# Attention values with the probabilities stationary: the product computed untransposed, scaled from PSUM and transposed once

## Chip, cores, metric

One core of a Trainium2 chip runs the whole kernel as one program. The metric is device time in microseconds, from launch to end; the median of three runs stands for a kernel. A profile is one execution recorded by the hardware profiler; its span runs from the first to the last instruction. PE is TensorE (PEld its weight loads), DVE VectorE, ACT ScalarE, POOL GpSimd, SP SyncE. All data is fp32; a matmul operand marked fp32r is an fp32 value rounded for the faster matmul form.

## What is computed

Two transformer-like models in a row on 512 tokens of width 1024. Four attention stages matter here, three kinds of token attention and one cross-attention into 256 memory tokens; the rest are projections, feed-forward blocks and a delta-rule stage. The stages differ in their scores and masks and end alike:

```python
def windowed_gqa(q, k, v, sink):           # 12 heads, blocks of 128 queries, 256 or 384 keys
...
    p = jax.nn.softmax(jnp.concatenate([s, sink_col], axis=-1), axis=-1)[..., :-1]
    o = jnp.einsum('bkgniu,bnukd->bnikgd', p.astype(v.dtype), vband)
def neighbourhood_attn(q, k, v, rpb):      # 12 heads, all 512 keys, a bias per pair of positions
...
    o = jnp.einsum('bhrcij,brijhd->brchd', p.astype(v.dtype), vband)
def memory_attn(q, k, v):                  # 4 heads, 256 memory keys
...
    o = jnp.einsum('bhsm,bmhd->bshd', p.astype(v.dtype), v)
def swa_mixer(h, wq, wk, wv, q_norm_w, k_norm_w, sinks, wo):   # 16 heads, 16 meta tokens first
...
    orr = (jnp.einsum('bnkgim,bmkd->bnikgd', p[..., :N_META], vm)
           + jnp.einsum('bnkgij,bnjkd->bnikgd', p[..., N_META:], vband))
```

The head width is 64. The result of each stage goes through an output projection.

## The kernel before

Activations lie transposed, features on partitions and tokens along the row. Large matmuls run in three passes of rounded halves (`h_hi`, `h_lo` against `w_hi`, `w_lo`, L949 and L962); attention values and transposes run in plain fp32.

An attention stage works on *pairs*: two heads of one feature tile and one block of queries. A pair is numbered by `count`; `slot` is its parity. Layer 0 has 24 pairs of windowed attention (blocks of 2, 3, 3 and 2 chunks of 128 keys) and 8 pairs of memory attention (2 chunks); layer 1 has 24 pairs of neighbourhood attention (4 chunks) and 8 memory pairs; the last layer has 40 pairs (8 tiles of 5 blocks: one of 16 queries by 16 keys, one of 128 + 16 keys, three of 128 + 128 + 16 keys).

Each engine has its own program, in an order written out by hand, and meets the others only through semaphores. The stage is a software pipeline: in step *p* PE does the scores of pair *p* (L1031), the values of pair *p*-2 (L1060) and the transposes of the probabilities of pair *p*-1 (L1044). A plain fp32 matmul is issued as two passes, each with its own weight load, so a chunk of values costs two passes per head, a transpose one.

For the values of a pair (`values`) PE keeps the values `v_st` (n keys by 64 columns) stationary and streams the transposed probabilities `p_t` (128 queries): the output has features on partitions, head 0 on partitions 0 to 63 and head 1 on 64 to 127 of PSUM bank 6 or 7. The reciprocals of the row sums lie with queries on partitions, so they must be turned as well: DVE computes `p_inv` (L1252), ACT spreads it to 64 columns a head (`spread`, L758, into `p_rec`), PE transposes it into the other half of the bank (L1064) and only then raises `pv_done`. ACT then copies the product to SBUF (`move_y`, L766, into `y_sb`), DVE multiplies it by the reciprocals in PSUM (`normalise`, L1237), ACT rounds the result into `h_hi` (`y_hi`, L771) and POOL computes the remainder `h_lo` (L579), which the output projection waits for. POOL also stages queries, keys and values for the next tile.

PE's step waits for `s_read` (scores bank free), `pt_ready` (probabilities turned and copied), `y_ready` (bank 6 or 7 free, a pair two earlier) and `rec_ready`. ACT's step is `move_y(p-2)`, `y_hi(p-3)`, and twice `turned(p-1)` and `probs(p)`, then `spread(p-1)`. DVE's step is the scale, bias and row maximum of pair *p* (L1232 or L1242, L1257), the reciprocal of *p*-1 and `normalise(p-2)`.

## Time and profile before

| | us |
|---|---|
| median of three runs | 3296.27 (3291.29 to 3299.48) |
| span of the profiled execution | 3296.4 |
| PE busy in it | 2886.2 (88%) |
| DVE, ACT, POOL busy | 1329.9, 981.6, 1204.4 |

The five attention stretches in the profiled execution, from their first score to the next stage's first matmul, read from the timeline: layer 0 tokens 174 to 254 us, memory 254 to 278; layer 1 tokens 888 to 984, memory 984 to 1008; last layer 2620 to 2812.6. The granted TensorE clock has two levels in this profile, shown as 1.00 (2.4 GHz) and 0.50 (1.2 GHz) of full speed; a stretch that holds both shows a mean. How to read a row of the stretch table: busy time and instruction count of each engine inside the stretch, then the mean granted clock.

### The profile page before, as it was taken

What the parts mean: (1) busy time and instruction counts of PE and PEld (TensorE: products, weight loads), DVE (VectorE), ACT (ScalarE), POOL (GpSimd) and SP (SyncE); (2) the same over time, 40 slices, a digit from 0 to 9 for tenths busy, and PEclk for the clock granted to TensorE, in tenths of its full rate; (3) what the DMA queues carried; (4) which work ended last, traced back from release to release, by engine and by line L of the source; (5) the groups of instructions that cost most, each with busy time, mean ns of one, the idle gap of its engine ahead of it and who ended that gap; (6) DMA issues with size and microseconds to landing.
All of it is one profiled execution on the core that took longest, in us unless ns stands there. A gap on an engine that the chain in (4) does not pass through costs nothing.

```text
span 3296.4 us, 50250 instructions
## 1 busy us (share of the span) xinstructions
PE 2886.2 (88%) x18018; PEld 2530.7 (77%) x18018; DVE 1329.9 (40%) x1506; ACT 981.6 (30%) x1863; POOL 1204.4 (37%) x727
## 2 busy tenths in 40 slices
PE   6898899989998999979966667999998699899998
PEld 5766778767976778759955556999998466799998
DVE  2265321341275322354724444653642233464361
ACT  3264212221284222232441113222222454322221
POOL 3443444434453434424321103433434132343342
PEclk7999999989999999989967787999998755899999
DMA  4211222322231222322200001222222000122222
GB/s 129 69 44 47 75 88 90 99 73 77 53 54 51 83 93 85 99 68 71 83 26 0 0 0 51 72 87 84 91 81 64 20 1 1 51 83 85 86 90 77
DMA packets 80355, 212.78 MB, mean 65 GB/s; under 512 B 30224, under 2 KB 32912, under 8 KB 80272
## 3 DMA queue, kind: packets, MB, share of 16 engines
q1 hardware_dynamic: 80272, 211.69, 21.0%
q8 instruction: 49, 0.80, 0.1%
q14 instruction: 34, 0.28, 0.0%
HBM read 209.57 MB, written 2.10 MB: 64 GB/s over the span
## 4 chain that ended last, share of the span: by engine, by line
PE 75%; DVE 8%; issue 7%; ACT 4%; POOL 4%; DVEq 1%; DMA 0%; POOLq 0%; ACTq 0%; SPq 0%
PE ps L949 56%; PE ps L1060 5%; PE ps L962 4%; PE ps L1136 3%; PE ps L1044 2%; POOL w_lo L486 2%; PE ps L1031 2%; DVE normed L1232 2%; POOL h_lo L620 2%; PE ps L1121 1%; DVE sq_sum L1237 1%; PE ps L1064 1%; DVE act_lo L1237 1%; ACT h_hi L726 1%; DVE n_max L1257 1%
## 5 line engine op out<-in xcount | busy, mean ns | idle before, releaser
L486 POOL TENSOR_TENSOR w_lo<-raw,w_hi 128x1024 fp32r<-128x1024 f32 (+1 forms) x352 | 896.6, 2549 | 1339.7 <-ACT w_hi L685 1339.7
L949 PE MATMUL ps<-h_hi,w_hi 128*128 128x264 f32 (+2 forms) x3120 | 826.8, 321 | 46.4 <-POOL w_lo L486 29.4
L685 ACT ACTIVATE w_hi<-raw 128x1024 fp32r<-128x1024 f32 (+1 forms) x352 | 392.4, 1116 | 1521.4 <-PE ps L949 1365.6
L949 PE MATMUL ps<-h_lo,w_hi 128*128 128x264 f32 (+2 forms) x3120 | 828.6, 322 | 0.0
L949 PE MATMUL ps<-h_hi,w_lo 128*128 128x264 f32 (+2 forms) x3120 | 826.8, 321 | 0.0
L949 PEld LDWEIGHTS ps<-h_hi,w_hi 128*128 128x128 f32 x3120 | 524.4, 191 | 95.1 <-POOL w_lo L486 32.8
L949 PEld LDWEIGHTS ps<-h_lo,w_hi 128*128 128x128 f32 x3120 | 522.2, 190 | 42.3
L949 PEld LDWEIGHTS ps<-h_hi,w_lo 128*128 128x128 f32 x3120 | 522.7, 191 | 41.5
L949 PE MATMUL ps<-act_hi,w_hi 128*128 128x264 f32 (+1 forms) x1056 | 289.6, 329 | 51.9 <-DVE act_lo L1237 51.9
L949 PE MATMUL ps<-act_lo,w_hi 128*128 128x264 f32 (+1 forms) x1056 | 289.1, 329 | 0.0
L949 PE MATMUL ps<-act_hi,w_lo 128*128 128x264 f32 (+1 forms) x1056 | 288.3, 328 | 0.0
L1237 DVE TENSOR_TENSOR x<-x,ps 128x512 f32 (+1 forms) x96 | 66.8, 696 | 474.6 <-PE ps L949 474.6
L949 PEld LDWEIGHTS ps<-act_hi,w_hi 128*128 128x128 f32 x1056 | 181.1, 194 | 71.0 <-POOL w_lo L486 54.3
L1060 PE MATMUL ps<-p_t,v_st 128*64 128x128 f32 (+1 forms) x1136 | 198.8, 332 | 12.6 <-ACT p_t L747 7.3
L1237 DVE TENSOR_TENSOR prod<-silu_g,ps 128x512 f32<-128x512 f32 (+1 forms) x88 | 61.3, 697 | 356.2 <-PE ps L949 303.7
L949 PEld LDWEIGHTS ps<-act_lo,w_hi 128*128 128x128 f32 x1056 | 181.3, 195 | 16.5
L949 PEld LDWEIGHTS ps<-act_hi,w_lo 128*128 128x128 f32 x1056 | 180.9, 194 | 16.0
L1237 DVE TENSOR_TENSOR sq_sum<-sq_sum,sq 128x512 f32<-128x512 f32 (+2 forms) x80 | 167.5, 2094 | 57.2 <-ACT sq L693 54.7
L1060 PEld LDWEIGHTS ps<-p_t,v_st 128*64 128x64 f32 (+1 forms) x1136 | 132.8, 162 | 73.7 <-issue 45.6
L1237 DVE TENSOR_TENSOR act_lo<-prod,act_hi 128x512 f32 (+1 forms) x88 | 155.0, 1761 | 22.1 <-DVE act_hi L1247 22.1
L1242 DVE TENSOR_SCALAR conv<-padded,vec 128x528 f32<-128x528 f32 x56 | 102.3, 1827 | 108.2 <-ACT padded L808 104.4
L1247 DVE CAST act_hi<-prod 128x512 f32 (+1 forms) x88 | 131.5, 1495 | 18.0 <-DVE prod L1237 18.0
(196 smaller groups left out, 3439.1 us busy)
## 6 DMA issues: line engine op xcount, KB each, us to landing
raw<-slabs_d SPq DMA_DIRECT2D x288, 512.0 KB, 3.5
raw<-slabs_d SPq DMA_DIRECT2D x64, 704.0 KB, 4.1
rpb_raw<-rpb_d SPq DMA_DIRECT2D x24, 224.0 KB, 5.0
bias_sb<-alibi_d SPq DMA_DIRECT2D x6, 384.0 KB, 3.3
x<-x_d SPq DMA_DIRECT2D x1, 2048.0 KB, 12.4
out_d<-x SPq DMA_DIRECT2D x1, 2048.0 KB, 7.0
mem_in<-mem_d SPq DMA_DIRECT2D x1, 1024.0 KB, 6.0
dn_cst<-dn_consts_d SPq DMA_DIRECT2D x1, 640.0 KB, 5.7
```

What stands on the lines that cost most here:

```text
L486: nc.gpsimd.tensor_tensor(w_lo[:, s, 0:size * P], raw[:, s, 0:size * P], w_hi[:, s, 0:size * P].bitcast(f32), ALU.subtract).then_inc(lo_do ...
L620: nc.gpsimd.tensor_tensor(h_lo[:, k, t], normed[:, k % 2, t], h_hi[:, k, t].bitcast(f32), ALU.subtract).then_inc(h_ready, 1)
L685: nc.scalar.activation(w_hi[:, s, 0:size * P], raw[:, s, 0:size * P], ACT.Copy).then_inc(hi_done, 1)
L949: last = nc.tensor.matmul(ps[:, s * 2 * BANK + po:s * 2 * BANK + po + n], w[:, s, wk], a[:, k, to:to + n], start=(k == 0 and w is w_hi and ...
L962: last = nc.tensor.matmul(out, a[:, k, t0:t0 + n], w[:, s, wk], start=(k == 0 and w is w_hi and a is h_hi), stop=(k == DT - 1 and w is w_lo))
L1031: last = nc.tensor.matmul(bank(2 * p.slot + h)[0:p.nq, col:col + n], a[hp, p.tile_slot, p.q], b[hp, p.tile_slot, k0:k0 + n], start=(b is k ...
L1044: last = nc.tensor.transpose(bank(4 + h)[0:n, j * P:j * P + p.nq], s_sb[0:p.nq, p.slot, h, 1 + col:1 + col + n], ident[0:p.nq, 0:p.nq])
L1060: nc.tensor.matmul(out[HD * h:HD * h + HD, 0:p.nq], v_st[0:n, p.tile_slot, vb, HD * h:HD * h + HD], p_t[0:n, h, j, 0:p.nq], start=(j == 0) ...
L1136: last = nc.tensor.matmul(out[:, h, :], lhs(h), rhs(h), start=start, stop=stop)
L1237: return nc.vector.tensor_tensor(*a, **kw)
L1242: return nc.vector.tensor_scalar(*a, **kw)
L1247: return nc.vector.tensor_copy(*a, **kw)
```

## The change

`values` swaps its operands: the transposed probabilities (n keys by 128 queries) are stationary and the values (64 columns) are streamed, so that the product has queries on partitions and both heads side by side. DVE multiplies it straight out of PSUM by `p_inv`, broadcast along each head's 64 columns, into `y_rows`; PE transposes `y_rows` once into the second half of the same bank (`turn_y`); ACT rounds that from PSUM into `h_hi`, and DVE, no longer POOL, computes `h_lo` from PSUM. `spread`, `move_y`, `p_rec`, `y_sb` and POOL's part are gone.

```diff
@@ POOL, attend @@
-                    pool.wait_ge(y_hi_ready, k + 1)
-                    nc.gpsimd.tensor_tensor(h_lo[:, st.y + i, q], y_sb[:, (i * nb + b) % 2, 0:c["nq"]],
-                                            h_hi[:, st.y + i, q].bitcast(f32), ALU.subtract).then_inc(y_lo_ready, 1)
@@ ACT, attend @@
-                def spread(p):
...
-                def move_y(p):
...
                 def y_hi(p):
-                    act.wait_ge(y_ready, p.count + 1)
-                    nc.scalar.activation(h_hi[:, st.y + p.tile, p.q], y_sb[:, p.slot, 0:p.nq],
+                    act.wait_ge(y_turned, p.count + 1)
+                    nc.scalar.activation(h_hi[:, st.y + p.tile, p.q], bank(6 + p.slot)[:, P:P + p.nq],
                                          ACT.Copy).then_inc(y_hi_ready, 1)
@@ PE, attend @@
                     if counted(p.count - 1):
-                        pe.wait_ge(y_ready, p.count - 1)
+                        pe.wait_ge(y_lo_ready, p.count - 1)
...
-                            nc.tensor.matmul(out[HD * h:HD * h + HD, 0:p.nq],
-                                             v_st[0:n, p.tile_slot, vb, HD * h:HD * h + HD],
-                                             p_t[0:n, h, j, 0:p.nq], start=(j == 0), stop=(j == len(cs) - 1))
-                    pe.wait_ge(rec_ready, p.count + 1)
-                    nc.tensor.transpose(out[:, P:P + p.nq],
-                                        p_rec[0:p.nq, p.slot, :],
-                                        ident[0:p.nq, 0:p.nq]).then_inc(pv_done, 1)
+                            last = nc.tensor.matmul(out[0:p.nq, HD * h:HD * h + HD],
+                                                    p_t[0:n, h, j, 0:p.nq],
+                                                    v_st[0:n, p.tile_slot, vb, HD * h:HD * h + HD],
+                                                    start=(j == 0), stop=(j == len(cs) - 1))
+                    last.then_inc(pv_done, 1)
+
+                def turn_y(p):
+                    pe.wait_ge(y_scaled, p.count + 1)
+                    nc.tensor.transpose(bank(6 + p.slot)[:, P:P + p.nq], y_rows[0:p.nq, p.slot, :],
+                                        ident[0:p.nq, 0:p.nq]).then_inc(y_turned, 1)
 
                 def step(p):
                     scores(p)
+                    if p.back(3).exists:
+                        turn_y(p.back(3))
                     if p.back(2).exists:
                         values(p.back(2))
@@ DVE, attend @@
-                    if counted(p.count - 1):
-                        wait(rec_ready, p.count - 1)
...
                 def normalise(p):
-                    wait(y_moved, p.count + 1)
-                    y = y_sb[:, p.slot, 0:p.nq]
-                    tt(y, y, bank(6 + p.slot)[:, P:P + p.nq], ALU.mult).then_inc(y_ready, 1)
+                    wait(pv_done, p.count + 1)
+                    wait(inv_ready, p.count + 1)
+                    tt(y_rows[0:p.nq, p.slot, :].rearrange("p (h n) -> p h n", h=2),
+                       bank(6 + p.slot)[0:p.nq, 0:P].rearrange("p (h n) -> p h n", h=2),
+                       p_inv[0:p.nq, p.slot, :].unsqueeze(2).to_broadcast([p.nq, 2, HD]),
+                       ALU.mult).then_inc(y_scaled, 1)
+
+                def y_lo(p):
+                    wait(y_hi_ready, p.count + 1)
+                    tt(h_lo[:, st.y + p.tile, p.q], bank(6 + p.slot)[:, P:P + p.nq],
+                       h_hi[:, st.y + p.tile, p.q].bitcast(f32), ALU.subtract).then_inc(y_lo_ready, 1)
...
+                    if p.back(3).exists:
+                        y_lo(p.back(3))
```

PE in a step of the windowed stage of layer 0 (scores of a pair with 256 keys, values of one with 3 chunks, transposes of one with 3 chunks); each values row is issued as two passes. Before:

```order
L1031 MATMUL ps<-k_hi,q_hi 128x256 [waits s_read]
L1031 MATMUL ps<-k_hi,q_hi 128x256
L1031 MATMUL ps<-k_lo,q_hi 128x256 x2
L1031 MATMUL ps<-k_hi,q_lo 128x256 x2
L1060 MATMUL ps<-p_t,v_st 64x128 [waits pt_ready]
L1060 MATMUL ps<-p_t,v_st 64x128 x2
L1060 MATMUL ps<-p_t,v_st 64x128 [waits pt_ready]
L1060 MATMUL ps<-p_t,v_st 64x128 x2
L1064 MATMUL ps<-cst,p_rec 128x128 [waits rec_ready]
L1044 MATMUL ps<-cst,s_sb 128x128 [waits pt_ready,p_ready]
```

And the same step of the changed kernel (L990 is the line of the scores, L1019 of the values, L1003 of the transposes, L1027 of `turn_y`):

```order
L990 MATMUL ps<-k_hi,q_hi 128x256 [waits s_read]
L990 MATMUL ps<-k_hi,q_hi 128x256
L990 MATMUL ps<-k_lo,q_hi 128x256 x2
L990 MATMUL ps<-k_hi,q_lo 128x256 x2
L1027 MATMUL ps<-cst,y_rows 128x128 [waits y_scaled]
L1019 MATMUL ps<-v_st,p_t 128x64 [waits pt_ready]
L1019 MATMUL ps<-v_st,p_t 128x64 x2
L1019 MATMUL ps<-v_st,p_t 128x64 [waits pt_ready]
L1019 MATMUL ps<-v_st,p_t 128x64 x2
L1003 MATMUL ps<-cst,s_sb 128x128 [waits pt_ready,p_ready]
```

The one transpose moved from behind the values to ahead of them and now belongs to a pair one step older; the values' output shape went from 64x128 to 128x64, in the same number of matmuls.

DVE in one step of the same stage, before:

```order
L1237 TENSOR_TENSOR s_sb<-rows 128x2 [waits pt_done]
L1232 SCALAR_TENSOR_TENSOR s_sb<-ps,bias_sb 128x2x384 [waits s_done]
L1257 TENSOR_REDUCE n_max<-s_sb 128x2
L1252 RECIPROCAL p_inv<-p_sum 128x2 [waits rec_ready,p_ready]
L1237 TENSOR_TENSOR y_sb<-y_sb,ps 128x128 [waits y_moved]
```

And of the changed kernel:

```order
L1204 TENSOR_TENSOR s_sb<-rows 128x2 [waits pt_done]
L1199 SCALAR_TENSOR_TENSOR s_sb<-ps,bias_sb 128x2x384 [waits s_done]
L1224 TENSOR_REDUCE n_max<-s_sb 128x2
L1219 RECIPROCAL p_inv<-p_sum 128x2 [waits p_ready]
L1204 TENSOR_TENSOR h_lo<-ps,h_hi 128x128 [waits y_hi_ready]
L1204 TENSOR_TENSOR y_rows<-ps,p_inv 128x128 [waits inv_ready,pv_done]
```

A sixth instruction came in ahead of the last one, and the last one waits for PE where it waited for ACT.

## Rows read from the trace of the kernel before

**Rows 1.** The page: granted TensorE clock in 40 equal slices, tenths.

```profile
PEclk7999999989999999989967787999998755899999
```

**Rows 2.** Stretches: busy us (instructions) of each engine, granted clock, DMA.

```profile
186.00:254.00 68.00, 63.10 (x487) 46.75 (x485) 47.07 (x105) 53.92 (x196) 30.56 (x48) 1.00 0.22 53
254.00:257.40 3.40, 1.27 (x13) 0.68 (x12) 2.76 (x4) 1.91 (x7) 3.23 (x6) 1.00 0.00 0
257.40:260.80 3.40, 3.40 (x21) 2.52 (x21) 2.00 (x5) 2.33 (x9) 0.85 (x2) 0.50 0.04 10
260.80:277.00 16.20, 14.86 (x116) 10.40 (x114) 9.61 (x22) 13.40 (x56) 2.75 (x6) 1.00 0.00 1
899.10:984.00 84.90, 84.18 (x715) 67.19 (x714) 62.09 (x89) 70.92 (x205) 50.81 (x58) 1.00 0.33 57
...
2636.50:2646.80 10.30, 9.61 (x76) 6.39 (x74) 4.86 (x16) 6.56 (x33) 6.32 (x11) 1.00 0.00 0
2646.80:2812.60 165.80, 162.42 (x722) 102.87 (x720) 59.46 (x167) 78.07 (x360) 39.69 (x76) 0.50 0.00 1
2812.60:2817.40 4.80, 4.77 (x22) 4.80 (x23) 0.00 (x0) 0.00 (x0) 0.00 (x0) 0.50 0.01 3
```

**Rows 3.** Stretches, L1105 alone (loads 128 columns, streams 8): PE, PEld, clock.

```profile
1670.00:1674.00 4.00, 4.00 (x38) 4.00 (x37) 0.99 0.00 0
1674.00:1684.50 10.50, 10.50 (x51) 10.50 (x51) 0.50 0.00 0
```

**Rows 4.** Timeline, layer 1, PE: start, us, instruction, count [idle before <- releaser].

```profile
932.10 0.33 PE L1064 MATMUL ps<-cst,p_rec 128*128 128x128 f32 x1
...
934.13 1.70 PE L1060 MATMUL ps<-p_t,v_st 128*64 128x128 f32 x16
935.76 0.33 PE L1064 MATMUL ps<-cst,p_rec 128*128 128x128 f32 x1
```

**Rows 5.** Timeline, layer 1, DVE in the same step.

```profile
934.28 1.23 DVE L1232 SCALAR_TENSOR_TENSOR s_sb<-ps,bias_sb 128x1024 f32<-128x1024 f32 x1 [0.38 <-PE ps L1031]
...
937.30 0.29 DVE L1237 TENSOR_TENSOR y_sb<-y_sb,ps 128x128 f32<-128x128 f32 x1
```

**Rows 6.** Timeline, layer 0, PE's transposes of the reciprocals in three steps.

```profile
219.45 0.33 PE L1064 MATMUL ps<-cst,p_rec 128*128 128x128 f32 x1
...
222.82 0.33 PE L1064 MATMUL ps<-cst,p_rec 128*128 128x128 f32 x1
...
225.79 0.33 PE L1064 MATMUL ps<-cst,p_rec 128*128 128x128 f32 x1
```

**Rows 7.** Timeline, layer 0, DVE: the first instruction of two successive steps.

```profile
218.54 0.16 DVE L1237 TENSOR_TENSOR s_sb<-rows 128x2 f32 x1 [0.17 <-issue]
...
221.80 0.16 DVE L1237 TENSOR_TENSOR s_sb<-rows 128x2 f32 x1 [0.17 <-issue]
```

**Rows 8.** Timeline, memory attention of layer 0, PE.

```profile
262.07 0.33 PE L1064 MATMUL ps<-cst,p_rec 128*128 128x128 f32 x1
264.68 0.33 PE L1064 MATMUL ps<-cst,p_rec 128*128 128x128 f32 x1
```

**Rows 9.** Chain that ended last, last layer: start, us, engine, tile, line, count.

```profile
2630.12 2.46 PE ps L1060 x8
...
2648.08 2.46 PE ps L1060 x8
...
2668.99 0.32 ACT s_sb L735 x2
...
2671.95 2.46 PE ps L1060 x8
...
2677.08 3.32 PE ps L1060 x12
...
2682.26 3.32 PE ps L1060 x12
```

**Rows 10.** Timeline, end of the last layer's attention, ACT's copy of the last product.

```profile
2810.65 0.28 ACT L766 ACTIVATE y_sb<-ps 128x128 f32<-128x128 f32 x1 [3.10 <-PE ps L1064]
```

More of the change, by code:

```diff
@@ L782, in step @@
                         probs(p, h)
-                    if p.back(1).exists:
-                        spread(p.back(1))
                 over_pairs(act.Fori, st, step)
                 last = last_pair(st)
-                move_y(last.back(1))
                 y_hi(last.back(2))
@@ L790, in attend @@
                     turned(last, h)
-                spread(last)
-                move_y(last)
                 y_hi(last.back(1))
@@ L1083, in attend @@
                 last = last_pair(st)
+                turn_y(last.back(2))
                 values(last.back(1))
                 turn(last)
+                turn_y(last.back(1))
                 values(last)
+                turn_y(last)
             def ffn(st):
@@ L1385, in attend @@
                 invert(last)
+                y_lo(last.back(2))
                 normalise(last.back(1))
+                y_lo(last.back(1))
                 normalise(last)
+                y_lo(last)
             def residual(q0, blk, squares):
```

47 lines of the change are left out of this document (11 added, 36 removed).

## The prediction

> **What bounds the kernel now.** I read the page first, then the stretch table, then single steps on the timeline. The page's clock line [rows 1] is near full speed except in three places; the 31st to 34th slice are the last layer's attention and what leads to it. The change touches only the attention steps, 104 pairs in about 410 of the 3296 us, so everything is decided there.
>
> PE bounds them, but at two clocks. In the token attention of layers 0 and 1 the clock is 1.00 and PE is busy 63.1 of 68.0 and 84.2 of 84.9 us. In the last layer it is 0.50 for 165.8 us although PE is busy 162.4 of them [rows 2]. So a busy PE does not raise the clock by itself; it matters what it does. The memory stage of layer 0 shows both directions: in the gap between two stages (PE busy 1.27 of 3.40) the clock falls, PE then works through 3.40 us at half clock, and the clock is back.
>
> **What a pass costs.** Today a pass of values loads 64 columns and streams 128; afterwards it loads 128 and streams 64. L1105 shows such a load-heavy pass: 128 columns of a 4-byte operand loaded, 8 streamed. At clock 0.99 it made 38 passes in 4.00 us (0.105 each), at 0.50 51 in 10.5 us (0.206) [rows 3]. Today's values pass costs (1.70 - 0.27) / 15 = 0.095 us at full clock, with some overlap of the two heads [rows 4]. So the halved stream buys nothing: the load of 128 columns takes its place, at both clocks. I take 0.105 and 0.21 for a pass of the changed kernel; from below the bound would be half of each (the stream alone), and rows 3 speak against that.
>
> The Trainium skill (TensorE: Matmul & The Clock Gate, section on LDWEIGHTS) gives a load as columns / 1.2 ns, whatever the clock: 107 ns for 128 columns. At full clock rows 3 agree; at half clock they show 206. By the page the last layer would save 0.1 us on each of its 352 full passes, 35 us.
>
> The count of passes stays: a values pass for a values pass, `turn_y` for the reciprocals' transpose. In layers 0 and 1 one change of the array's shape per step goes, about 0.1 us, and layer 1 loses the overlap of the two heads, 16 x (0.105 - 0.095), about 0.16. PE's work per step is the same within 0.1 us.
>
> **What happens to the clock.** This is the term that decides. L1105 loads full width, streams 8 columns, is back to back, busy 4.00 of 4.00 us, and the clock falls within it and stays at 0.50 for 10.5 us of unbroken work [rows 3]. Loads, then, do not hold the clock; streaming does. The change halves what the values stream: a memory pair streams (8 x 128 + 5 x 128 + scores) today and (8 x 64 + 5 x 128 + scores) afterwards. The last layer's pairs, with a third of their values passes on 16 rows, stream little for their time and stay at half clock for 165.8 us. Afterwards memory pairs and two-chunk pairs of layer 0 are in the last layer's place: when a gap between stages has dropped the clock, I expect nothing to raise it before the output projection. Three-chunk pairs may raise it, four-chunk pairs (layer 1) should.
>
> The Trainium skill (the same page, Part 1) says that sustained matmul activity releases the throttle and that idle time brings it back. By that rule a PE that never idles would keep the full clock after the change too: it is the first rival below. The last layer contradicts it (162.4 of 165.8 us busy at 0.50) and so does L1105.
>
> **Price of a pair at half clock.** A three-block step of the last layer takes 2682.26 - 2677.08 = 5.18 us [rows 9] for 19 passes (12 values, 6 transposes, 1 reciprocals): 19 x 0.21 = 4.0; three scores of 272 columns at 1.2 GHz, 0.68; the rest, 0.5, are six changes of the array's shape. With two changes left, a pair of layer 0 with 3 chunks costs 4.0 + 0.96 + 0.16 = 5.1, one with 2 chunks 13 x 0.21 + 0.64 + 0.16 = 3.5, one of layer 1 25 x 0.21 + 1.28 + 0.16 = 6.7. Today they take 3.37 and 2.97 (mean 3.17) [rows 6], a memory pair 2.61 [rows 8], a pair of layer 1 935.76 - 932.10 = 3.66 [rows 4].
>
> **The sum**, against the profiled 3296.4, which is the median within 0.2:
>
> 1. Layer 0 tokens: half clock for none to all of 24 pairs, each (5.1 + 3.5) / 2 - 3.17 = +1.15: 0 to 28. I take half of them: **+13.8**.
> 2. Two memory stages: 8 x (3.5 - 2.61) = 7.3, less 0.9 for the 3.4 us that already run at half clock, less about 1 for pairs of the stage's start and end that wait anyway: 5.5 each, **+11**.
> 3. The output projections behind them then start at half clock, as the last layer's does now for 4.8 us [rows 2]: half of that, twice, **+4.8**.
> 4. Layer 1 tokens: 3.4 us more at half clock after the start, x (1 - 3.66 / 6.7): **+1.6** (0 to 40, were it never to rise).
> 5. The last layer loses its one stretch at full clock, 10.3 us [rows 2]. The period that holds it took 2648.08 - 2630.12 = 17.96, the next 23.87 [rows 9]: **+5.9**.
> 6. DVE gets `y_lo`, 0.29 us by the row of the same shape, and a wait before it (0.1 to 0.25), less one wait in the reciprocal: +0.4 a step. In layer 1 DVE's chain is 937.30 + 0.29 - 934.28 = 3.31, with 0.1 to the next start 3.4, and it waits 0.38 for PE [rows 5]; with 3.8 it is longer than PE's 3.66: 24 x 0.15 = **+3.6**. In layer 0 its step with 384 keys takes 3.26 [rows 7] of 3.37; with 3.66 it adds 0.29 on the six such pairs still at full clock: **+1.7**. At half clock DVE is hidden behind PE. Ends: 0 (the added operation hides in the wait) and 12.
> 7. ACT loses `spread` and `move_y`, some 0.5 us a step. In layer 0 its step and PE's transpose of the reciprocals form the loop of 3.37, so PE is released from it; DVE's 3.66 takes over. In the last layer ACT stands on the chain for 0.32 us once in a period [rows 9], 8 periods, of which I credit 0.25: **-2**. At the end of a stage that a projection follows, the chain loses the copy, 0.28 us [rows 10], and a hop between engines, about 0.2: thrice, **-1.5**. POOL's release gains nothing: PE waits for it only at a stage's start.
>
> Together +38.9: **3335 us**, 1.2% slower.
>
> **The rivals.**
>
> A. *The clock holds* in layers 0 and 1 and the memory stages (the page's rule, or a margin larger than I think). For it: four-chunk pairs have much to give away, and today's memory stage regains the clock after one 3.4 us stretch. Against it: rows 3 and the last layer. Then terms 1 to 4 vanish, term 6 is 3.6 + 12 x 0.29 = 7, term 5 perhaps stays: 3296 + 7 + 6 - 3.5 = 3306 down to 3300. Chance 0.12.
>
> B. *Full-width loads are cheap at half clock* (the page's figure for LDWEIGHTS) while the clock falls as forecast: 35 us come back in the last layer and about 10 in the other half-clock pairs: 3335 - 40 = 3295, no change. Chance 0.05.
>
> C. *Both*: the clock holds and loads hide. At full clock DVE bounds anyway, so the last layer's 35 us are the gain: 3303 - 35 = 3268. Chance 0.07.
>
> D. *DVE's early link*: PE now waits for `y_scaled` of pair p-3 right behind the scores, where it waited for a product a whole step older. If that ties PE's step to DVE's (3.8 and 3.7 plus two hops of 0.2 in two steps, 3.95 each), layer 1 adds 24 x 0.15 more and layer 0 about 2: 3340, inside the forecast's range. It decides only where DVE's step is as long as PE's, not at half clock.
>
> E. *Layer 1 falls too* and stays at half clock: + up to 24 x 3.0 = 72, near 3400. Its pairs still stream most of all attention pairs. Chance 0.04.
>
> **Chances and range.** The forecast with D's variant has 0.72, and by its own ends (term 1 from 0 to 28, the rest as summed) runs from 3315 to 3360. The rest is A 0.12, B 0.05, C 0.07, E 0.04. The range 3300 to 3360 takes in A and leaves C and E out. A measurement of this kernel tells about 0.3% (10 us, so 3286 and 3306) from no change. Faster is C with a sliver of B: 0.08. Same is A and B: 0.15. Slower is the forecast and E: 0.77.
>
> **What the profile of the changed kernel would show.** Term 1 to 4: the stretches of layer 0, above all both memory stages, with a granted clock of 0.50 and PE busy nearly throughout; the output projections' first microseconds at 0.50. Term 5: no stretch at 1.00 between the last layer's first score and its projection. The pass: values with 0.21 us from start to start at half clock, 0.105 at full; 0.11 at half clock would prove B. Term 6: in layer 1 DVE busy nearly without waiting for PE, steps of 3.8 us. I am wrong if the memory stages run at 1.00 (then 3300 to 3306) or if layer 1's steps are shorter than 3.66 us.

## The result and the profile after

The changed kernel takes 3352.83 us (median of 4, 3348.04 to 3356.12), the kernel before 3293.94 beside it: a ratio of 1.0172, 95% interval 1.0158 to 1.0186. It is 1.7% slower, 58.9 us by the medians and 57.9 by the spans of the two profiled executions (3354.3 against 3296.4). The forecast was 38.9 us. Two of the ten executions of a later kernel (e5) took 3302.0 and 8825.3 us at a lower granted clock (0.897 and 0.298, against 0.912 to 0.918) and are left out of its ratio.

The page of the changed kernel, granted TensorE clock in 40 slices, answers [rows 1]:

```profile
PEclk7875999998997999998986778899998755799999
```

The third and fourth slice, where layer 0's attention and its projection stand, are new, and so is the 7 in the thirteenth, layer 1's memory stage. The next view gives the five attention stretches, from the first score of a stage to its last product: us, then for each engine busy time and instructions, granted clock, DMA share, GB/s. First the kernel before, cut at the same places (layer 0 tokens, layer 0 memory, layer 1 tokens, layer 1 memory, last layer):

```profile
174.50:253.30 78.80, 71.52 (x530) 52.82 (x530) 55.55 (x119) 59.59 (x214) 39.95 (x55) 0.96 0.19 46
253.30:277.50 24.20, 20.71 (x153) 14.43 (x152) 14.65 (x32) 18.11 (x72) 6.91 (x13) 0.93 0.01 2
889.30:983.10 93.80, 90.12 (x746) 71.47 (x746) 69.30 (x95) 74.79 (x214) 60.11 (x65) 0.98 0.30 51
983.10:1007.60 24.50, 20.66 (x153) 14.54 (x152) 14.64 (x32) 18.11 (x72) 6.90 (x13) 0.93 0.00 1
2619.80:2810.60 190.80, 183.71 (x856) 116.96 (x856) 75.60 (x198) 90.65 (x421) 55.35 (x98) 0.53 0.02 6
```

And the changed kernel:

```profile
181.70:284.70 103.00, 95.89 (x528) 81.48 (x528) 62.25 (x143) 51.04 (x168) 33.45 (x38) 0.62 0.15 35
284.70:317.80 33.10, 31.03 (x153) 26.07 (x152) 17.00 (x40) 15.27 (x57) 0.00 (x0) 0.50 0.00 1
930.10:1036.40 106.30, 96.04 (x746) 80.08 (x746) 76.36 (x119) 64.21 (x168) 54.04 (x48) 0.97 0.27 45
1036.40:1069.10 32.70, 30.30 (x152) 25.46 (x152) 17.01 (x40) 15.27 (x56) 0.00 (x0) 0.54 0.00 1
2677.40:2870.60 193.20, 187.77 (x856) 145.79 (x856) 85.61 (x238) 75.23 (x344) 40.22 (x60) 0.50 0.02 6
```

Two different losses stand side by side. In layer 0 and in both memory stages TensorE is busy nearly all the time, at a lower clock: +24.2, +8.9 and +8.2 us. In the tokens of layer 1 the clock is what it was (0.97), and TensorE is idle 10.3 us of 106.3 where it was idle 3.7 of 93.8: +12.5 us. Not all of that is waiting: TensorE's busy time there rose by 5.9 us (90.12 to 96.04), at nearly the same clock, because its passes and steps are a little longer; e5 below shows what that costs. The last layer, at half clock before as well, adds 2.4. The two output projections take 46.2 and 46.0 us instead of 44.7 each, since they start at half clock: +2.8.

One more difference has nothing to do with attention. A stretch of 96 passes of the memory keys and values, the same in both kernels, ran at full clock before and mostly at half after (before, then after):

```profile
60.00:71.00 11.00, 10.92 (x96) 10.78 (x96) 0.47 (x2) 1.40 (x2) 4.75 (x2) 1.00 0.39 103
60.00:78.20 18.20, 18.10 (x96) 17.91 (x95) 0.49 (x2) 1.27 (x3) 4.73 (x2) 0.57 0.24 87
```

That is 7.3 us in this one execution. Of the twelve kernels run later, with the same code there, one (e5) shows it slow and eleven fast. So it belongs to the execution, and the change's own loss in the profile is nearer to 50 than to 58 us. The medians can't be corrected for it, as each kernel has a profile of one execution only.

In layer 0 the clock does not stay down from the stage's start. From 193.7 to 211.7 us it is at 1.00, with TensorE busy 14.6 of 18.0 us, and it falls to 0.50 at about 216 us, inside the stage and with no gap between stages before it. It stays there for the 68.7 us that are left of the tokens and through the memory stage.

A pass at half clock costs what rows 3 said. TensorE, changed kernel, memory stage of layer 0 (start, us, line, form, count), answers [rows 8]:

```profile
297.55 0.48 PE L1027 MATMUL ps<-cst,y_rows 128*128 128x128 f32 x1
297.82 1.81 PE L1019 MATMUL ps<-v_st,p_t 128*128 128x64 f32 x8
299.42 1.06 PE L1003 MATMUL ps<-cst,s_sb 128*128 128x128 f32 x4
...
301.35 0.48 PE L1027 MATMUL ps<-cst,y_rows 128*128 128x128 f32 x1
```

Eight value passes from 297.82 to 299.42 are 0.20 us each, and the pair takes 301.35 - 297.55 = 3.80 us (2.61 before, 3.5 forecast). In layer 1 at full clock (answers [rows 4]):

```profile
962.90 0.33 PE L1027 MATMUL ps<-cst,y_rows 128*128 128x128 f32 x1
963.08 2.00 PE L1019 MATMUL ps<-v_st,p_t 128*128 128x64 f32 x16
...
967.43 0.33 PE L1027 MATMUL ps<-cst,y_rows 128*128 128x128 f32 x1 [0.59 <-DVE y_rows L1204]
```

and VectorE over two steps, from 959.21 on (answers [rows 5]):

```profile
959.21 1.22 DVE L1199 SCALAR_TENSOR_TENSOR s_sb<-ps,bias_sb 128x1024 f32<-128x1024 f32 x1 [0.20 <-PE ps L990]
...
961.84 0.17 DVE L1219 RECIPROCAL p_inv<-p_sum 128x2 f32<-128x2 f32 x1
962.10 0.29 DVE L1204 TENSOR_TENSOR h_lo<-ps,h_hi 128x128 fp32r<-128x128 f32 x1
...
963.32 1.23 DVE L1199 SCALAR_TENSOR_TENSOR s_sb<-ps,bias_sb 128x1024 f32<-128x1024 f32 x1 [0.48 <-PE ps L990]
964.64 1.22 DVE L1224 TENSOR_REDUCE n_max<-s_sb 128x2 f32<-128x1024 f32 x1
966.07 0.17 DVE L1219 RECIPROCAL p_inv<-p_sum 128x2 f32<-128x2 f32 x1 [0.21 <-issue]
966.63 0.29 DVE L1204 TENSOR_TENSOR h_lo<-ps,h_hi 128x128 f32 x1 [0.40 <-issue]
967.08 0.29 DVE L1204 TENSOR_TENSOR y_rows<-ps,p_inv 128x128 f32<-128x128 f32 x1 [0.16 <-issue]
967.64 1.23 DVE L1199 SCALAR_TENSOR_TENSOR s_sb<-ps,bias_sb 128x1024 f32<-128x1024 f32 x1 [0.27 <-issue]
```

Two VectorE steps take 967.64 - 959.21 = 8.43 us, 4.2 each, where TensorE's step was 3.66. The last 3.0 us of them hold no wait for another engine, and TensorE waits 0.59 us for what comes out of them. The first of the two steps still belongs to the group that the kernel writes out ahead of its loop, the second to the loop. The remainder `h_lo` follows the reciprocal within 0.1 us in the first and after 0.40 us in the second.

Two theories come out of this, and they need not exclude each other. **Clock**: the value passes stream half the columns, and that is what lost the clock. **VectorE**: with the remainder in its sequence VectorE sets the step at full clock. A variant of it says that it is the place of `y_rows` in the chain, not the length of the sequence (rival D of the prediction).

### The profile page after: what moved, and what is told of

It is laid out like the page before. It is cut to its first block, busy times and chain, and to the rows that moved or that the text cites. A ratio compares the mean times of both kernels' runs of the same rounds, so it can differ in the third digit from the quotient of the medians.

```text
span 3354.3 us, 49859 instructions
## 1 busy us (share of the span) xinstructions
PE 2943.8 (88%) x18018; PEld 2623.1 (78%) x18018; DVE 1357.5 (40%) x1610; ACT 939.8 (28%) x1655; POOL 1159.4 (35%) x623
## 4 chain that ended last, share of the span: by engine, by line
PE 75%; DVE 9%; issue 7%; ACT 4%; POOL 4%; DVEq 1%; DMA 0%; POOLq 0%; ACTq 0%; SPq 0%
PE ps L908 55%; PE ps L1019 5%; PE ps L921 4%; PE ps L1103 3%; PE ps L1003 2%; PE ps L990 2%; POOL w_lo L485 2%; DVE normed L1199 2%; POOL h_lo L602 2%; PE ps L1088 1%; DVE sq_sum L1204 1%; DVE n_max L1224 1%; DVE s_sb L1199 1%; PE ps L1027 1%; DVE act_lo L1204 1%
## 5 line engine op out<-in xcount | busy, mean ns | idle before, releaser
L1019 PE MATMUL ps<-v_st,p_t 128*128 128x64 f32 (+1 forms) x1136 | 227.2, 361 | 4.7 <-ACT p_t L731 4.5
L1019 PEld LDWEIGHTS ps<-v_st,p_t 128*128 128x128 f32 (+1 forms) x1136 | 212.1, 270 | 21.8 <-issue 5.3
```

The source lines that it names most:

```text
L1019: last = nc.tensor.matmul(out[0:p.nq, HD * h:HD * h + HD], p_t[0:n, h, j, 0:p.nq], v_st[0:n, p.tile_slot, vb, HD * h:HD * h + HD], start=( ...
```

## The experiments

Ratios are to the kernel before, run beside each kernel. Its medians in the four sets were 3297.0, 3298.3, 3297.6 and 3298.3 us, so the kernels' times can be compared across sets.

### e1: the columns of both heads

```diff
-                            last = nc.tensor.matmul(out[0:p.nq, HD * h:HD * h + HD],
+                            last = nc.tensor.matmul(out[0:p.nq, P * (2 + h):P * (3 + h)],
                                                     p_t[0:n, h, j, 0:p.nq],
-                                                    v_st[0:n, p.tile_slot, vb, HD * h:HD * h + HD],
+                                                    v_st[0:n, p.tile_slot, vb, :],
```

(and `normalise` reads the half of each head that counts)

> The changed kernel, with one thing else: each value pass streams the 128 columns of both heads' values instead of the 64 of its own head, and the half that belongs to the other head is left unread. The number of passes and what they load stay. Theory (the clock): the pairs of layer 0 and of both memory stages ran at half clock (granted clock 0.50 from 216 to 289 and from 289 to 318.8 us in the changed kernel) because the value passes stream half the columns; with 128 columns again these stretches are back at 1.00 for the most part, a pass still takes about 0.11 us at full clock (16 in 2.00 us), layer 0's attention takes 105 to 115 us instead of 136.0, and the kernel 3305 to 3325. What is left above the kernel before is the chain over VectorE. Rival (the clock goes by the time that TensorE is busy, or by passes): the half-clock stretches stay where they are and the kernel is within 8 us of 3353. Second rival: twice the columns make a pass longer; then 16 value passes of layer 1 take over 3 us and the kernel is slower than 3353.

Measured: **3314.0 us** (ratio 1.0048, 1.0033 to 1.0063), 38.8 below the changed kernel and 17.0 above the kernel before. The profiled execution is the slowest of its ten (3324.3 us, granted clock 0.899 where most had 0.903), so some 10 us of the stretches below are not in its median; which stretch holds them is not known. The five stretches again:

```profile
174.10:264.10 90.00, 66.28 (x528) 54.91 (x528) 64.15 (x143) 51.93 (x168) 33.41 (x38) 0.96 0.17 40
264.10:290.60 26.50, 20.82 (x153) 16.81 (x152) 17.02 (x40) 15.18 (x56) 0.00 (x0) 0.87 0.01 1
901.50:1006.40 104.90, 95.38 (x744) 79.74 (x744) 76.38 (x119) 64.17 (x168) 54.07 (x48) 0.98 0.28 46
1006.40:1032.40 26.00, 19.88 (x153) 16.27 (x152) 17.02 (x40) 15.19 (x56) 0.00 (x0) 0.93 0.00 1
2641.40:2838.50 197.10, 190.20 (x856) 136.22 (x856) 86.54 (x238) 74.73 (x343) 40.24 (x60) 0.56 0.02 6
```

Layer 0's attention, 116.5 us with its memory stage, just misses the forecast of 105 to 115. The instructions are the same in number, but for a few records that the traces miss. Only what each value pass streams, and writes to PSUM, has doubled, and the clock is back, from 0.62 to 0.96, 0.50 to 0.87 and 0.54 to 0.93. At full clock a pass costs hardly more: 16 take 1.88 us (933.03 to 934.91 on the timeline) where the changed kernel's take 1.74 to 1.83. At half clock it costs 0.03 us more, 8 in 1.86 us (269.23 to 271.09) for 1.60, and so the last layer, which stays near half clock, gets 3.9 us longer (197.1 for 193.2). So the columns streamed (with what they write) are the cause, not busy time and not the number of passes or loads: TensorE was busy 95.89 of 103.0 us at a clock of 0.62 and is busy 66.28 of 90.0 at 0.96. This speaks directly against the rule of the Trainium skill (TensorE: Matmul & The Clock Gate, Part 1) that the clock goes by how busy TensorE has been, if busy is what the profile counts as busy.

What is left above the kernel before, 90.0 against 78.8 us in layer 0's tokens and 104.9 against 93.8 in layer 1's, is now visible without the clock. VectorE in layer 0 of e1:

```profile
203.08 0.16 DVE L1204 TENSOR_TENSOR s_sb<-rows 128x2 f32 x1 [0.18 <-issue]
203.39 0.96 DVE L1199 SCALAR_TENSOR_TENSOR s_sb<-ps,bias_sb 128x768 f32<-128x768 f32 x1
204.44 0.95 DVE L1224 TENSOR_REDUCE n_max<-s_sb 128x2 f32<-128x770 f32 x1
205.55 0.17 DVE L1219 RECIPROCAL p_inv<-p_sum 128x2 f32<-128x2 f32 x1 [0.16 <-issue]
205.94 0.29 DVE L1204 TENSOR_TENSOR h_lo<-ps,h_hi 128x128 f32 x1 [0.22 <-issue]
206.47 0.29 DVE L1204 TENSOR_TENSOR y_rows<-ps,p_inv 128x128 f32<-128x128 f32 x1 [0.23 <-issue]
206.94 0.16 DVE L1204 TENSOR_TENSOR s_sb<-rows 128x2 f32 x1 [0.18 <-issue]
```

It waits for no engine at all. The step is 206.94 - 203.08 = 3.86 us; [rows 7] has 3.26 for the same step before. VectorE is the bound there, and TensorE waits for it: in the stage's 90.0 us it waits 21 times, 21.1 us in all, at `turn_y` for `y_rows`.

### e2 and e3: the transpose of the rows behind the values

```diff
                     scores(p)
-                    if p.back(3).exists:
-                        turn_y(p.back(3))
                     if p.back(2).exists:
                         values(p.back(2))
+                    if p.back(3).exists:
+                        turn_y(p.back(3))
```

(and on VectorE `normalise(p-2)` ahead of `y_lo(p-3)`); e2 on the changed kernel, e3 on e1.

> The changed kernel, in another order: TensorE transposes the scaled rows of pair p-3 behind the value passes of pair p-2 instead of ahead of them, and VectorE scales pair p-2 before it takes the remainder of pair p-3. The same instructions. Theory (the chain over VectorE costs about 10 us in layer 1: there, at full clock, PE sat idle 0.4 to 0.6 us before each transpose of y_rows, and the stretch of 84.9 us became 95.6): the idle time ahead of that transpose goes, layer 1 loses 8 to 10 us, and the kernel takes 3341 to 3347. Layer 0, at half clock, has no such idle time and stays at 136 us. Rival (VectorE's own added work, not its place in the chain, sets the step of layer 1): the idle time moves to another instruction and the kernel stays at 3350 to 3356.

> The two edits together: value passes that stream both heads' 128 columns, and the transpose of the scaled rows behind the value passes. If the clock and the chain over VectorE are all of the loss, the kernel is back within 10 us of the kernel before: 3290 to 3306, with layer 0's attention at 100 to 106 us (102.9 before) and layer 1's at 116 to 122 (118.3 before). If something else takes part (the remainder on VectorE, the 7.3 us that the second half of the memory keys' and values' projection lost), it stays above 3306.

Measured: e2 **3370.7 us** (1.0198, 1.0157 to 1.0239), e3 **3334.1** (1.0106, 1.0069 to 1.0143). e2 missed both of its ranges, and e3 is above 3306, as its second theory had it. Each is slower than the kernel it was made from, by 18 and 20 us. At full clock the chain is not shortened but moved. In e3's layer 1:

```profile
935.33 2.05 PE L1019 MATMUL ps<-v_st,p_t 128*128 128x128 f32 x16 [0.53 <-DVE h_lo L1204]
```

TensorE waits ahead of the values instead, because the bank is free only after the remainder. In e2 layer 1 with its memory stage takes 139.5 us, 139.0 in the changed kernel.

Layer 0's attention takes 147.8 us in e2 (136.1 in the changed kernel). Its tokens:

```profile
173.40:285.00 111.60, 109.90 (x520) 94.28 (x520) 61.65 (x141) 50.73 (x167) 33.02 (x37) 0.51 0.14 33
```

TensorE hardly waits there. What is lost is clock, 0.51 where the changed kernel has 0.62 (181.7 to 284.7 us). Why the clock was down here from the first microseconds of the stage on stays open; one of its four executions took 3358.6 us, 12 less than the others, so it may differ between executions.

So the early place of `turn_y` was not the main trouble. In e3 moving it gave layer 1 three microseconds (128.0 for 130.9) and cost the last layer eight (204.8 for 197.1). Of the 20 us between the medians of e3 and e1 the profiles show only 6 (3328.5 and 3322.5), because e3's is of its fastest execution and e1's of its slowest; the rest is not located.

### e5: e1 without the remainder on VectorE

The low part of the attention's output is left out, which computes less than the reference.

```diff
                     if p.back(1).exists:
                         invert(p.back(1))
-                    if p.back(3).exists:
-                        y_lo(p.back(3))
```

(and the waits for `y_lo_ready` become waits for `y_hi_ready`)

> The kernel of e1 (value passes stream both heads' 128 columns) without VectorE's remainder: the attention's output has no low part, h_lo of these rows isn't written, and what waited for it waits for the rounded part; so this computes less than the reference. It prices the remainder. In e1 VectorE runs layer 0 without waiting for any engine: from 203.39 to 207.25 us one step of 3.86 us, of which the remainder takes 0.29 and the gap before it 0.22 to 0.40. Theory (at full clock VectorE's sequence of five or six instructions sets the step): a step gets 0.45 to 0.65 us shorter, layer 0's attention goes from 116.5 to 102 to 107 us, layer 1's from 130.9 to 117 to 121, and the kernel from 3314 to 3285 to 3296. Rival (the chain through y_rows and its transpose sets it, whatever VectorE has to do besides): less than 8 us of 3314 come back.

Measured: **3260.8 us** (0.9872, 0.9858 to 0.9886), 53 below e1. The stretches of tokens in layer 0, tokens in layer 1, and of the last layer:

```profile
181.70:262.20 80.50, 66.46 (x528) 55.40 (x528) 58.69 (x120) 50.52 (x168) 33.48 (x38) 0.96 0.19 45
...
894.40:993.50 99.10, 95.64 (x746) 80.86 (x746) 69.64 (x96) 64.02 (x168) 53.98 (x48) 0.95 0.30 49
...
2625.40:2775.50 150.10, 140.02 (x856) 101.69 (x856) 80.70 (x200) 73.47 (x343) 40.28 (x60) 0.82 0.03 8
```

With their memory stages the attention of layer 0 takes 104.2 us (forecast 102 to 107) and that of layer 1 122.6 (117 to 121). The tokens got back 9.5 of the 11.2 us that e1 had lost in layer 0, and 5.8 of the 11.1 in layer 1. One instruction of 0.29 us a step, with the gap before it, is most of the loss at full clock in layer 0. In layer 1 it is half. The other half is TensorE's own: it is busy 95.64 of 99.10 us in e5, and a step in which it waits for nothing takes 957.28 - 953.46 = 3.82 us on the timeline, where it took 3.66 [rows 4]; sixteen value passes take 1.79 us of it (1.63 before). A pass of e5, like one of e1 and of the changed kernel, loads 128 columns; the kernel before loads 64. The last layer was not forecast: 150.1 us where e1 had 197.1, with the clock at 0.82 for 0.56, and so the kernel came out below the forecast of 3285 to 3296. Its clock goes up and down all through the stage, where e1's stays at 0.50 for the first 140 us. TensorE's matmuls are the same in both, so VectorE's sequence, or the waits that hang on it, also acts on the clock. How it does so no run here separates.

### e6 and e10: ScalarE scales the rows

```diff
+                def scale_y(p):
+                    act.wait_ge(pv_done, p.count + 1)
+                    act.wait_ge(inv_ready, p.count + 1)
+                    for h in range(2):
+                        done = nc.scalar.activation(
+                            y_rows[0:p.nq, p.slot, HD * h:HD * h + HD],
+                            bank(6 + p.slot)[0:p.nq, 2 * P + 3 * HD * h:2 * P + 3 * HD * h + HD],
+                            ACT.Copy, scale=p_inv[0:p.nq, p.slot, h:h + 1])
+                    done.then_inc(y_scaled, 1)
```

In e6 it is called at the end of ScalarE's step, in e10 ahead of `turned(p-1)`; both on e1.

> The kernel of e1 with the scaling of the rows moved from VectorE to ScalarE (two activations of 64 columns each, with the reciprocal as the scale, at the end of ScalarE's step). Everything is computed. Theory (VectorE's sequence sets the step at full clock): it loses an instruction of 0.29 us and the gap of 0.16 before it, ScalarE has room (59.6 of 93 us busy in e1's layer 1), so a step takes 3.8 us in layer 1 instead of 4.1 to 4.3: layer 0's attention 105 to 109 us, layer 1's 120 to 124, kernel 3292 to 3302. Rival (the chain through y_rows): ScalarE scales later than VectorE did, so the transpose of y_rows comes later, and the kernel stays at 3314 or above.

> The kernel of e6, one thing moved: ScalarE scales pair p-2 ahead of its copies of pair p-1's transposes, not at the end of its step. In e6 TensorE sat idle 1.41, 1.68 and 1.46 us before three successive transposes of y_rows, while ScalarE had been idle 0.86 us ahead of those copies. Theory (e6 was slow because the scaling stood at the end of ScalarE's step and everything on TensorE is queued behind that transpose): these waits end, the attention of layer 0 takes 102 to 108 us (141.5 in e6), that of layer 1 118 to 124 (179.8), the kernel 3288 to 3302. Rival (ScalarE's work as such is too long in this design): above 3340.

Measured: e6 **3452.1 us** (1.0456, 1.0438 to 1.0473), e10 **3321.7** (1.0073, 1.0045 to 1.0100). e6 is the dearest kernel of the study. Its timeline, TensorE in layer 0:

```profile
231.24 0.33 PE L1041 MATMUL ps<-cst,y_rows 128*128 128x128 f32 x1 [1.41 <-ACT y_rows L744]
```

Here rival D's mechanism is real: values, transposes and scores are all queued behind this one transpose, and it waits for the end of ScalarE's step, which waits for TensorE. Scaling earlier took 130 us back, but e10 is still not below e1, and 20 above its forecast. Its tokens did gain (85.1 us in layer 0, 98.9 in layer 1, against 90.0 and 104.9). Everything is computed in it, and VectorE is relieved of the scaling where e5 relieves it of the remainder. Its layer 1, at 98.9 beside e5's 99.1, says the same as e5's. In layer 0 it gained less than forecast, because TensorE there waits for the remainder before the values:

```profile
PEld ps L1033 <- DVE h_lo L1218: 10.2, 12, 1.3
```

The last layer took it back (202.6 for 197.1, clock 0.53).

### e4, e8, e12: the kernel before, its last layer

Its clock of 0.50 was there before the change, so it was worth asking what holds it down.

```diff
+                        nc.gpsimd.memset(v_st[:, :, 4, :], 0.0)
+                        nc.gpsimd.memset(p_t[:, :, 0:3, :], 0.0)
...
                         for j, (_, n, vb) in enumerate(cs):
+                            n = P if n == META else n
                             nc.tensor.matmul(out[HD * h:HD * h + HD, 0:p.nq],
```

> The kernel before, with the last layer's value passes of the 16 meta keys widened: the rows 16 to 127 of that chunk of the values are zero, and the pass goes over all 128 rows. Three facts of the last layer of the kernel before speak to it: granted clock 0.50 for 180.7 of 191 us, 8 value passes in 2.46 us and 12 in 3.32. Theory (passes over 16 rows count little for the clock, and each change of the array's shape costs): the stretch at half clock shrinks or ends, the 12 passes take under 2.8 us even at half clock, and the kernel takes 3225 to 3280. Rival (rows don't matter for the clock, only the change of shape costs 0.15 to 0.2 us): the clock stays at 0.50 and 32 steps with 4 changes each give 19 to 26 us, so 3268 to 3277. Second rival (neither): within 5 us of 3294.

e8 widens the transposes of the chunk and ScalarE's copies too (VectorE clears `s_sb` once at the stage's start):

```diff
                         for j, (col, n, _) in enumerate(p.c["chunks"]):
+                            n = P
                             last = nc.tensor.transpose(bank(4 + h)[0:n, j * P:j * P + p.nq],
...
-                    full = sum(1 for ch in cs if ch[1] == P)
+                    full = len(cs)
```

> The kernel of e4 (the kernel before, meta chunk of the values over 128 rows) with the transposes of that chunk widened to 128 columns too and ScalarE's two copies of a head's transposed probabilities made one. Theory (each change of the array's shape costs TensorE 0.15 to 0.2 us, and the 16-row copy costs ScalarE 0.25 us a head): a step of the last layer, 2.8 us in e4, gets 0.2 to 0.4 us shorter, 32 times: 3209 to 3216. Rival (another engine sets the step there, ScalarE's chain for the reciprocals): within 4 us of e4's 3221.9.

e12 keeps the narrow passes and adds one wide product per head that nobody reads:

```diff
+                        if st.bias == "band" and p.nq == P:
+                            nc.tensor.matmul(out[HD * h:HD * h + HD, 2 * P:3 * P],
+                                             v_st[:, p.tile_slot, cs[0][2], HD * h:HD * h + HD],
+                                             p_t[:, h, 0, :], start=True, stop=True)
```

> The kernel before, with its narrow passes kept, and one more pass per head in the last layer's steps of 128 queries: it repeats the first chunk's value pass (128 rows, 128 columns streamed) into columns of the bank that nobody reads. It is work that computes nothing, 2 passes a step. It tells whether e4 gained because the array streams more on full rows or because the four changes of its shape per step were gone, since here they all remain. Theory (what is streamed on full rows holds the clock): the last layer comes to full clock for the most part, its attention takes 120 to 150 us instead of 190.9, the kernel 3226 to 3258, although TensorE does more. Rival (the changes of shape keep the clock down): the clock stays near 0.50 and the 64 or so added passes of 0.21 us make the kernel 3305 to 3312.

Measured: e4 **3221.9 us** (0.9769, 0.9731 to 0.9807), e8 **3219.1** (0.9756, 0.9738 to 0.9773), e12 **3295.9** (0.9995, 0.9983 to 1.0008). The last layer's attention in e4 (its start, then the rest) and in e12:

```profile
2616.00:2627.50 11.50, 6.52 (x44) 4.59 (x44) 9.61 (x13) 4.26 (x21) 10.04 (x12) 0.50 0.29 94
2627.50:2732.20 104.70, 98.02 (x814) 72.75 (x813) 64.59 (x185) 84.42 (x400) 45.23 (x86) 1.00 0.00 1
```

```profile
2616.60:2803.50 186.90, 177.84 (x984) 111.98 (x984) 75.37 (x198) 89.95 (x422) 55.39 (x98) 0.64 0.02 7
```

e4 takes 74.6 us off 190.8, with the same 856 passes, and **beats both kernels**, by 2.3% against before and 3.9% against the changed one. It is 3 us below its forecast of 3225 to 3280. Twelve passes take 1.49 us in a step where they took 3.32 [rows 9]. e11 below makes the same edit in a kernel whose clock hardly follows, and gains 26.4 us; by that some 48 of the 74.6 us are the clock (an estimate, as the two designs differ). e8's additions bring nothing that can be told from e4 (rival: another engine sets the step; its ScalarE has 2.5 us less to do and the stretch is 115.4 us for 116.2).

e12 fell between its theories. Streaming more, with the four changes of shape a step kept, raises the clock from 0.53 to 0.64; the stretch is 3.9 us shorter although it holds 128 passes more (two for each of the 64 products of the expectation, fp32 products being issued as two passes). So what is streamed counts in the kernel before too, but extra passes do not do what full rows do. Whether the rest is that narrow rows count for less, or that the changes of shape take time in which nothing is streamed, these two kernels can't separate.

### e7, e9, e11: the same edit in the changed design

e11 is the changed kernel, e9 is e1, each with e4's edit; e7 is e6 with e8's.

```diff
                         for j, (_, n, vb) in enumerate(cs):
+                            n = P if n == META else n
                             last = nc.tensor.matmul(out[0:p.nq, HD * h:HD * h + HD],
```

> The changed kernel as it is (value passes stream 64 columns) with the edit of e4 alone. It tells whether the changed design, too, gets the full clock in the last layer once its narrow passes are gone. Theory (no: what the value passes stream is too little there, as in layer 0 and the memory stages): the clock stays at 0.50 in the last layer, only the changes of the array's shape go, its attention takes 165 to 182 us instead of 193.2, the kernel 3328 to 3345. Rival (the narrow passes alone held the clock down): the last layer falls to 120 to 135 us and the kernel to 3280 to 3298.

> The kernel of e1 (value passes stream both heads' columns, VectorE scales) with the edit of e4 (the last layer's meta chunk of the values over 128 rows). With the clock near full everywhere, this is the price of the change without its clock: to be set beside e4 (3221.9 us). Theory (VectorE's longer sequence costs 0.4 to 0.6 us a step wherever the clock is full): the last layer's attention falls from 197.1 to 118 to 132 us and the kernel from 3314 to 3236 to 3252, 14 to 30 us above e4. Rival (the last layer's clock needs more than full rows in this design): above 3270.

> The kernel of e6 with the last layer's chunk of 16 meta keys made full: its transposes take 128 columns, ScalarE copies all chunks in one instruction, the rows 16 to 127 of the values are zero and the value pass goes over 128 rows. Theory (in the last layer the clock is low because of these narrow passes, in either design): the last layer's attention falls from about 195 to 110 to 120 us, and the kernel to 3212 to 3230. Rival (the changed design streams less in its value passes even so, or VectorE bounds it): above 3240. The comparison with e8, which has the same edits on the kernel before, says what the change itself is worth once the clock is out of it: I expect 5 to 15 us in favour of the kernel before.

Measured: e11 **3323.6 us** (1.0073, 1.0052 to 1.0095), e9 **3253.6** (0.9869, 0.9843 to 0.9896), e7 **3373.9** (1.0223, 1.0197 to 1.0249). The last layer's attention in e11 and in e9:

```profile
2669.80:2836.60 166.80, 158.04 (x856) 130.43 (x856) 88.30 (x238) 75.35 (x343) 40.30 (x60) 0.54 0.02 7
2636.30:2766.30 130.00, 101.48 (x856) 81.25 (x856) 87.01 (x238) 75.04 (x343) 40.38 (x60) 0.95 0.03 9
```

The same edit, the same number of passes: with 64 columns streamed the clock stays at 0.54, with 128 it is 0.95. That repeats e1 in a third kind of stage. It also prices the changes of shape. In e11 the clock hardly moves (0.50 to 0.54) and the stretch loses 193.2 - 166.8 = 26.4 us. Twelve value passes at half clock, first in the changed kernel, then in e11:

```profile
2786.43 3.23 PE L1019 MATMUL ps<-v_st,p_t 128*128 128x64 f32 x12
```

```profile
2783.49 2.66 PE L1022 MATMUL ps<-v_st,p_t 128*128 128x64 f32 x12
```

To the start of the transposes behind them (2789.59 and 2785.94) it is 3.16 and 2.45 us, 0.71 less for four changes of shape, nearly 0.2 each. In 32 steps with a narrow chunk that is 23 us; the rest is the clock and the other passes. The stretch came out inside its forecast (165 to 182 us), the kernel 4 us below its own (3328 to 3345). The Trainium skill (TensorEngine Tiling (Array Packing), Key Properties) says that a change of the tiling mode drains the engine; it gives no time, and e11 shows one.

e9 beside e4 is the price of the change with the clock nearly out of it (e9's five stretches are at 0.93 to 1.00, e4's at 0.93 to 1.00 as well): 3253.6 against 3221.9, **+31.7 us**, more than the 14 to 30 forecast. e7 (forecast 3212 to 3230) can't serve for that comparison, because it is built on e6 and carries e6's chain: its last layer, at 0.87, takes 169.8 us with TensorE busy 115.50 of them.

## Why the prediction was right, and where it was not

The direction and the range (3300 to 3360) held. The likeliest value was 18 us low. By its own steps, each measured in the profiled executions: steps 1, 2 and 4 as changed kernel against e1, step 6 as e1 against before, the others as changed kernel against before:

| step | forecast | measured |
|---|---|---|
| a pass of values at half and full clock | 0.21, 0.105 | 0.20, 0.11 |
| 1 layer 0 tokens, clock | +13.8 | +13.0 |
| 2 memory stages, clock | +11 | +13.3 |
| 3 output projections start at half clock | +4.8 | +2.8 |
| 4 layer 1 tokens, clock | +1.6 | +1.4 |
| 5 last layer loses its full clock, with ACT's relief | +3.9 | +2.4 |
| 6 VectorE's remainder, layers 0 and 1 | +5.3 (0 to 12) | +26.1, of which +20.6 by e5 |
| 7 tails of three stages | -1.5 | about -2.9 |

**Steps 1 to 4 held**: 31.2 forecast, 30.5 measured. The main reasons held as well: unbroken work at half clock, loads that do not hold the clock, and the Trainium skill's rule (rival A) not what decides here. Two things went otherwise. The prediction had the clock dropped by a gap between stages, with nothing to raise it; in layer 0 it did rise, and fell inside the stage. And the extent was more than I took: 16 of 24 pairs of layer 0 ran at half clock, not 12, at 68.7 / 16 = 4.3 us each as forecast. Step 1 still came out right because those pairs lost less than forecast: from the ninth transpose of `y_rows` to the end of the stage the changed kernel takes 284.7 - 218.8 = 65.9 us and e1 264.1 - 210.6 = 53.5, so 0.8 us a pair and not 1.15. At full clock such a pair would not have taken 3.37 or 2.97 us but VectorE's 3.86 or 3.49. That these two misses offset each other is luck. In step 2 a memory pair took 3.80 us and not 3.5. The price of a change of shape, 0.5 / 6 in the prediction, is nearly 0.2 us by e11.

**Step 6 was the one that failed**: it was put at 5.3 us and measured 26.1, with two errors in VectorE's part and one in TensorE's. The sequence grew by 0.6 us a step and not 0.4. In the loop's steps the instruction takes 0.29 us and has a gap of 0.21 to 0.40 before it. The forecast took the gap for the price of a wait, 0.1 to 0.25; but the same instruction with the same wait has under 0.1 us before it in the steps written out ahead of the loop (962.10 above). So the gap goes with the loop, whose steps reckon counts and addresses as they run; that this is what takes the time is not shown. Second, I charged the step only where a row showed VectorE longer than TensorE, for six pairs of layer 0 and 0.15 us a step in layer 1. But VectorE's 3.26 stood 0.11 below a step of 3.37 [rows 6, 7], so nearly every tenth added comes out again, in all 24 pairs, those with two chunks (3.49 us for 2.97) and the memory pairs too. The 26.1 is 11.2 and 11.1 for the tokens, 2.3 and 1.5 for the memory stages. The bound of 12 for the upper end had the same flaw. The rows for a better sum were there: slack 0.11 of 3.37 in layer 0, 0.38 of 3.66 in layer 1.

Third, not all of the 26.1 is VectorE's. Taking the remainder out (e5) gives back 9.5 and 5.8 us of the tokens and 2.8 and 2.5 of the memory stages, 20.6 together. What stays is mostly 5.3 us of layer 1, TensorE's own step of 3.82 us for 3.66. The prediction had that step the same within 0.1 us.

By the medians the split is another one: e1 is 17.0 us above the kernel before and 38.8 below the changed kernel, where by the spans of the profiled executions it is 26.1 above and 31.8 below. The larger cause is the same, and step 6 is over its forecast either way, but its measured 26.1 may be several microseconds too high.

**Steps 1 and 6 are not independent.** At half clock VectorE is hidden, at full clock it sets the step. The table adds up to 56.1 only because the clock's share is read against a kernel that VectorE already bounds; against a kernel with neither loss the clock alone should be dearer, which no run shows.

**Rival D** was given 0.15 us a step more than step 6, as a chain through `y_rows`. That is 3.6 us in layer 1 and 2 in layer 0. e3 takes this link away, and 2.9 us come back in layer 1 and 0.4 in layer 0 (116.1 for 116.5); its own wait, for the remainder, stands in the same place. e5 leaves the link and takes the remainder, and 20.6 come back. So in the changed kernel the link is mostly where a sequence that is too long shows. e6 shows what it costs when it does bind.

**Rivals A, B, C, E** did not come: the clock fell, a pass that loads 128 columns took 0.20 us at half clock and not 0.11, and the tokens of layer 1 stayed at 0.97.

What stays open beside e12's question is 5.5 us by which the rest of the kernel came out shorter in the changed kernel's profile (57.9 against the table's 56.1 and the 7.3 of the memory keys, in stretches of 1 to 2 us). Unchanged stretches can move by that much between kernels: the second output projection took 46.3 us in e4, whose code there is the kernel before's, and 44.7 in the kernel before. I did not separate them.

## What to carry to other kernels

Here, swapping a matmul's stationary and streamed operand left the pass at about the price of its load, and still lost whole stages their clock, because what the passes stream changed. So look at the granted clock of a stage beside its busy time, and at the columns and rows its passes stream, before taking a busy TensorE for a fast one. Where a stage sits at half clock though it is busy, try widening narrow passes with zero rows (75 us for three lines here) or with columns that nobody reads (39 us); extra passes that nobody reads gained nothing (e12). And before giving an engine one more small instruction, compare its step with the bound's step: with a slack of 0.1 us nearly all of it, the gap before it included, was paid in every step.

## What was not expected of the hardware

- Streaming 128 columns in place of 64, with half the result thrown away, cost a value pass next to nothing at full clock (0.12 us against 0.11; 0.23 against 0.20 at half) and made layer 0's tokens 13.0 us shorter.
- A pass over 16 rows is worse than one over 128 with 112 rows of zeros: 0.2 us for each change of the array's shape at half clock, and the clock besides (e4: 0.53 to 0.95).
- Taking one instruction a step from VectorE, with the waits for it, raised TensorE's clock in the last layer from 0.56 to 0.82 (e1 to e5) with the same matmuls, in one profiled execution of each.
- A small VectorE instruction cost about twice its own time in the loop, 0.29 us of work and 0.21 to 0.40 of gap, and hardly more than its own time with the same wait in the steps written out ahead of the loop (gap under 0.1).
- The full clock was lost inside a stage, at about 216 us in layer 0 of the changed kernel, with no gap between stages before it.
